# Moving four small SBUF tensors and dropping a 96-byte pad in a four-layer fp32 block kernel

## The reference

```python
x = x + even_layer(x, ...)   # rmsnorm, project to 9224 columns, banded attention + mLSTM, gates, project back
x = x + odd_layer(x, ...)    # rmsnorm, project to 6160 columns, RG-LRU + gated delta rule, gates, project back
h = _layer_ab(x, ...)        # rmsnorm, project to 8192, dilated attention + differential attention, gate, project back
h = _layer_c(h, ...)         # rmsnorm, project to 8192, causal attention of 16 heads, gate, project back
return _rmsnorm(h, final_norm)
```

## Time and profile before

| | |
|---|---|
| median of 3 runs | 2025.14 us (2023.06 to 2025.92) |
| profiled execution's own time | 2025.92 us |
| its span, first to last instruction | 2024.1 us |
| mean granted TensorE clock | 0.988 |
| TensorE busy | 1956.5 us, 97% |
| VectorE, ScalarE, GpSimd busy | 57%, 49%, 7% |
| weight DMA queue, share of 16 engines | 50.4% |

### The profile page before, as it was taken

The page is one execution under the profiler, slowest core; times in us unless marked ns, Lnnn a source line. Parts: engine busy times, 40 slices in busy tenths (PEclk is TensorE's granted clock), DMA queues, the critical chain, the costliest instruction groups (busy, mean ns, idle before and its releaser), DMA issues.

```text
span 2024.1 us, 29038 instructions
## 1 busy us (share of the span) xinstructions
PE 1956.5 (97%) x12004; PEld 1743.6 (86%) x12004; DVE 1163.0 (57%) x1655; ACT 994.4 (49%) x1525; POOL 145.7 (7%) x132
## 2 busy tenths in 40 slices
PE   7999989999999989899999999999999999999997
PEld 7987778888899979789889999988889989988886
DVE  4444454445555687848556646655556655655554
ACT  5344344565455645474553344456554344445643
POOL 0000010011001020120001101100100100100010
PEclk9999999999999989999999999999999999999999
DMA  7554445455554433435565554555555555554463
GB/s 258 164 192 146 146 139 196 154 166 172 186 170 147 128 122 126 146 105 167 186 198 183 185 174 154 166 182 157 178 171 183 190 188 168 165 181 157 161 208 125
DMA packets 172850, 338.51 MB, mean 167 GB/s; under 512 B 9536, under 2 KB 9920, under 8 KB 172592
## 3 DMA queue, kind: packets, MB, share of 16 engines
q1 hardware_dynamic: 171632, 332.89, 50.4%
q0 software_dynamic: 944, 3.61, 0.7%
q10 hardware_dynamic: 144, 0.17, 0.0%
HBM read 334.55 MB, written 2.10 MB: 166 GB/s over the span
## 4 chain that ended last, share of the span: by engine, by line
PE 84%; DVE 7%; issue 4%; ACT 4%; DMA 0%; POOL 0%; SPq 0%; DVEq 0%; ACTq 0%; POOLq 0%
PE ACC L643 16%; PE ACC L645 16%; PE ACC L644 16%; PE ACC L650 10%; PE ACC L651 10%; PE ACC L652 10%; DVE WL L1252 2%; ACT WH L951 1%; DVE S L1476 1%; PE PM L750 1%; PE PM L666 1%; PE PM L738 1%; PE PM L771 1%; ACT S L970 1%; PE PM L773 1%
## 5 line engine op out<-in xcount | busy, mean ns | idle before, releaser
L1252 DVE TENSOR_TENSOR WL<-RAW,WH 128x1024 fp32r<-128x1024 f32 x624 | 779.6, 1258 | 686.0 <-ACT WH L951 683.7
L951 ACT ACTIVATE WH<-RAW 128x1024 fp32r<-128x1024 f32 x626 | 656.2, 1054 | 509.1 <-PE ACC L645 284.6
L650 PE MATMUL ACC<-XH,WH 128*128 128x256 f32 x1920 | 556.1, 290 | 1.9 <-DVE WL L1252 1.9
L652 PE MATMUL ACC<-XH,WL 128*128 128x256 f32 x1920 | 545.3, 284 | 0.0
L651 PE MATMUL ACC<-XL,WH 128*128 128x256 f32 x1920 | 545.3, 284 | 0.0
L643 PE MATMUL ACC<-WH,XH 128*128 128x512 f32 x1024 | 416.6, 407 | 3.7 <-DVE WL L1252 3.7
L645 PE MATMUL ACC<-WH,XL 128*128 128x512 f32 x1024 | 401.5, 392 | 0.0
L644 PE MATMUL ACC<-WL,XH 128*128 128x512 f32 x1024 | 401.1, 392 | 0.0
L650 PEld LDWEIGHTS ACC<-XH,WH 128*128 128x128 f32 x1920 | 370.7, 193 | 3.8 <-DVE WL L1252 2.1
L651 PEld LDWEIGHTS ACC<-XL,WH 128*128 128x128 f32 x1920 | 370.7, 193 | 1.0
L652 PEld LDWEIGHTS ACC<-XH,WL 128*128 128x128 f32 x1920 | 370.2, 193 | 0.0
(11 more groups left out here) (328 smaller groups left out, 1683.0 us busy)
## 6 DMA issues: line engine op xcount, KB each, us to landing
RAW<-in_ev_w_in SPq DMA_DIRECT2D x71, 1024.0 KB, 4.9
RAW<-in_w_in_ab SPq DMA_DIRECT2D x64, 1024.0 KB, 5.3
RAW<-in_w_in_c SPq DMA_DIRECT2D x64, 1024.0 KB, 5.3
RAW<-in_od_w_in SPq DMA_DIRECT2D x48, 1024.0 KB, 5.1
RAW<-in_ev_w_out SPq DMA_DIRECT2D x16, 1024.0 KB, 4.9
RAW<-in_od_w_out SPq DMA_DIRECT2D x16, 1024.0 KB, 4.9
RAW<-in_w_out_ab SPq DMA_DIRECT2D x16, 1024.0 KB, 5.0
RAW<-in_w_out_c SPq DMA_DIRECT2D x16, 1024.0 KB, 4.9
```

The lines of the kernel that those rows point to most:

```text
L650: e.matmul(o, wh, xh, start=f and g % 2 == 0, stop=False, skip_group_check=True)
L652: m = e.matmul(o, wl, xh, start=False, stop=l, skip_group_check=True)
L951: e.activation(hi, src, ACT.Copy).then_inc(s_hi)
L1252: e.tensor_tensor(lo, src, hi.bitcast(F32), ALU.subtract).then_inc(s_lo)
```

## The change

The allocation calls of `VC`, `RB` and `SM` move from in front of `X` to behind `C`, and `PAD` goes. Nothing else differs: no instruction, wait, shape or order.

```diff
-        VC = sb("VC", VW)
-        RB = sb("RB", RW)
-        SM = sb("SM", 224)
-        PAD = sb("PAD", 24)
         X = sb("X", 2 * D)
         Y = sb("Y", 2 * D)
         XH = sb("XH", KT * 256, F32R)
...
         SC = sb("SC", 4096)
         C = sb("C", CW)
+        VC = sb("VC", VW)
+        RB = sb("RB", RW)
+        SM = sb("SM", 224)
         S5 = sb("S5", 2048)
         S6 = sb("S6", 2048)
         S0 = sb("S0", 2048)
```

## The result

The kernel after took 2035.88 us (median of 4 runs, 2035.19 to 2036.77) against 2025.43 us for the kernel before: ratio 1.0054, 95% interval 1.0037 to 1.0072. The change costs 10.4 us. The forecast was 2025.2 us with a range up to 2030.5 us, and slower had a chance of 0.16, so the time lies outside the forecast's range.

The account below looks back on a forecast made before the run. It took TensorE to bound the kernel, busy 1956.5 of 2024.1 us. 2025.92 us plus 0 for matmuls, VectorE and ScalarE, steady DMAs and start gave 2025.9, stated as 2025.2 us near the median before; range 2021.0 to 2030.5 us.

Parts of the forecast that it names:

- Matmuls of family (a): Over 10,300 of 12,004 matmuls with operands among X to C, moved to 128 bytes past 4096: 0, at most 5.0 us.
- The lower bound: Matmuls: a stream already moving a column a clock, 0.42 ns, has nothing to gain from other addresses: 0.
- Family (b): S0 to S6 and YH/YL, moved to 96 bytes short of 4096; 1,536 output-projection matmuls load YH/YL as stationary operand: 0.
- The sign that the prediction named for being wrong: Moving side of the array: it would fetch in blocks larger than the shift; no row covered it.
- VectorE, ScalarE, steady DMAs, start: Side engines' work, steady weight loads and first loads: 0 each; for the start, bounds of -0.2 and +1.8 us kept.
- The estimate of 6% and 1.3 us: Start's loads: 2 KB runs 128 bytes off a 256 multiple need 6% more beats, 1.3 us over the first 20 us.
- The row of VC: Load into VC, before 128 bytes past a multiple of 4096: 165 KB in 2.7 us, read as no address price.
- Rival 1: Every matmul: the moving operand pays for its start, 0.42 ns each, 5.0 us in all, to 2030.2 us; chance 0.13.
- Rival 2: Attention and recurrence steps: equal phases had cost VectorE and ScalarE something, 5.1 us faster, to 2020.0 us; chance 0.11.

Follow-up runs that it names:

- e4: Kernel before with PAD of 32 columns in place of 24, every tensor from X on 32 bytes past a multiple of 4096: 2025.40 us, ratio 0.9999.
- e10: Kernel after with an unused 224-byte tensor behind SM, so X to C and S0 to YLB have equal phases again: 2026.72 us, ratio 1.0001.
- e2: Kernel after with an unused 96-byte tensor behind SM, putting S0 to S6 and YHA to YLB back on multiples of 4096: 2034.27 us, ratio 1.0046.
- e3: Kernel after with an unused 32-byte tensor behind SM, S0 to S6 and YHA to YLB 64 bytes short of a multiple of 4096: 2036.05 us, ratio 1.0053.
- e1: Kernel before with an unused 32-byte tensor behind C, moving only S0 to S6 and YHA to YLB: 2036.44 us, ratio 1.0056.
- e6: Kernel before with only XH and XL moved, to 32 bytes past a multiple of 4096: 2024.31 us, ratio 0.9992.
- e8: Kernel before with XH and XL cut from one tensor, both starting 16 bytes past a multiple of 4096: 2020.34 us, ratio 0.9973.
- e9: Kernel before with WH and WL of 1088 columns, pieces of mode feat placed 224 bytes into the buffer, others at column 0: 2012.54 us, ratio 0.9929.

## Why the prediction was wrong, point by point

*What bounds the kernel.* Right. The chain and its shares are the same, the idle times of VectorE and ScalarE grew only by 7.8 and 7.0 us, and the loss arose in the engine that sets the end, so all of it was seen.

*Matmuls of family (a): 0.* Right for these addresses, since a family that moves as one keeps its phases (e4, and L642 and L649 after). Three reasons given for it were wrong. The lower bound said that a stream which moves a column a clock has nothing to gain: the slope is right (0.2267 less 0.1200 us over 256 columns is 0.417 ns), but each matmul carries some 13 ns on top of its columns (226.7 - 512 x 0.417, 120.0 - 256 x 0.417), so there was something to gain. Whether the phase changes this remainder or the pace of the columns isn't shown: at phase 224 the two widths take 233.3 and 118.3 ns, which on a line is 0.45 ns a column and 3 ns on top. A small spread doesn't prove that an operation is at its floor. And L638 and L811 as rows for odd starts measured a stationary operand of 8 to 32 columns; what pays in the runs is a load of 128 columns beside a long stream.

*Family (b): 0.* This is the step that failed. The prediction held the shift of YH and YL against rows of single odd addresses and took 0, at most a column or 0.42 ns a matmul. It measured about 6 ns for each of the 1536 (389 to 395 ns, and 227 to 233 ns from start to start), a factor of 14 above the bound, and that is the 10 us. The right question was not where an operand starts but where the two that are read together start; the sentence "within a family all distances stay" had the quantity in hand, and the output projections are the place where a wide product takes its two operands from two families. The sign that the prediction named for being wrong, a moving operand fetched in blocks larger than the shift, looked at one operand as well; e4 and e10, with all moving operands shifted, cost nothing.

*VectorE, ScalarE, steady DMAs, start: 0 each.* Right in the total: e10, which differs from the kernel before in all these starts, is at 1.0001. L1250 stands at 1257 ns against 1258, L949 at 1057 ns both times, landing of weights 5.2 us at the median against 5.1 us, first wait for a buffer ended 0.6 us earlier. One thing shows at the start when all sixteen traces are laid side by side. In the first 25 us, where the DMA engines are busy 93 to 95%, the five kernels whose X, RAW and C start off a multiple of 256 bytes (after, e2, e3, e4, e10) moved 328 to 335 GB/s, the eleven others 338 to 345. e1, on such multiples, and e10, off them:

```profile
0.00:25.00 25.00, 15.87 (x113) 1.00 0.94 341
```

```profile
0.00:25.00 25.00, 15.05 (x104) 1.00 0.95 333
```

The means are 332 and 341 GB/s, some 2.5% apart, or 0.6 us of 25; no run moved RAW, X or C off such a multiple by itself, so which of them pays isn't shown. The first wait of ScalarE doesn't follow it (it ended between 22.16 and 22.89 us in the five, between 21.89 and 22.95 us in the others), nor do the totals of e4 and e10. The estimate of 6% and 1.3 us, from the Trainium skill's rule on descriptors that start off a multiple of 256 bytes (DMA: Bandwidth & Descriptors, How a descriptor splits into AXI transactions), has the sign of these rates and more than twice their size. The row of VC, by which the prediction found no price, couldn't have shown it: VC keeps the same start modulo 256 bytes in every kernel here and landed in 2.3 to 2.8 us.

*Rivals.* Rival 1 had the sign but not the mechanism: it let the moving operand pay for its own start, on all matmuls, and e4 and e10 refute it. Rival 2 saw that the families stand 224 bytes apart after and looked for the effect in VectorE and ScalarE and as a gain. Its idea, that equal phases cost something, holds for the 256-column matmuls (e6, e8, e9), which the change leaves at equal phases. In the chances, 0.11 for faster engines and 0.02 for the median make 0.13 and not 0.12, which changes nothing in the forecast.

*What stays open.* That the two reads get in each other's way in SBUF is an inference from the overlap in the timeline and from the dependence on phase; no run shows the memory itself. The Trainium skill (TensorE: Matmul & The Clock Gate, Step-by-step: what each phase is for) says that TensorE reads the moving operand and the weight load through two independent ports, so that loading the next weights takes no bandwidth from the running matmul. The runs agree that the two overlap, and don't fit with full independence: the same pair takes 389 or 395 ns by their phase alone. Why the sign turns between 256 and 512 columns isn't known. The two narrow products, with 256 columns moving past a stationary operand of 16 or 32 columns, didn't share the gain of the wide ones: L638, 276 ns before, has 279 ns in e6. The side matmuls between S and SC in plain float32 also changed phase, and their means stayed, 378 ns before and after; whether that is the operand type or their order wasn't tried. Before, then after:

```profile
L771 PE MATMUL PM<-S,SC 128*128 128x256 f32 x24 | 7.1, 378 | 0.0
```

```profile
L769 PE MATMUL PM<-S,SC 128*128 128x256 f32 x24 | 7.1, 378 | 0.0
```

## What to carry to other kernels

When a change moves tensors, write down for every overlapped pair on the bounding engine the start addresses modulo 256 bytes of both operands, not whether each is aligned; a pad of a few columns, or an offset inside the buffer, sets the phase without an instruction more. Long streams of matmuls with a weight load for each were fastest here with equal phases at 512 columns and with 32 to 64 bytes of difference at 256 columns: 0.7% of the whole kernel for e9's edit of buffer sizes and slices. Which phase is good has to be measured for the width at hand. And an experiment that shifts everything together is a cheap way to tell "where" from "relative to what".

## What was unexpected of the hardware

- The phase modulo 256 bytes between moving and stationary operand changes a 512-column matmul from 226.7 to 233.3 ns from start to start and a 256-column one from 120.0 to 116.7 ns.
- 16 bytes of phase are enough for most of the gain at 256 columns (281 ns against 284) but only for part of the loss at 512 (395 ns, between 392 and 397; e8).
- A shift of all tensors together is without effect on the matmuls and on the time: e4, with every tensor from X on at 32 bytes past a multiple of 4096, is at 0.9999 (0.9989 to 1.0009).
- Loads into tensors that start off a multiple of 256 bytes went at a rate some 2.5% lower in the first 25 us, where the DMA engines were busy 93 to 95% (328 to 335 GB/s in five kernels against 338 to 345 in eleven), and the kernel's time didn't show it.
